# Block 1's projections as Strassen pairs ahead of attention, its gates kept in DRAM

## The reference

```python
u = _rmsnorm(h, norm_mix_g[l])
z = jnp.einsum('bsd,dn->bsn', u, w_in[l])
q, k, v, pz, ga, gp = jnp.split(z, offs, axis=-1)      # 768, 768, 768, 768, 1024, 1024 columns
a = _attention_branch(q, k, v).astype(dt)              # 12 heads of 64, dilations 1, 4, 16
p = _pool_branch(pz, w_pool_grp[l], pool_scale[l]).astype(dt)
merged = (jax.nn.sigmoid(ga) * jnp.einsum('bsc,cd->bsd', a, w_att_out[l])
          + jax.nn.sigmoid(gp) * jnp.einsum('bsc,cd->bsd', p, w_pool_out[l]))
h = h + jnp.einsum('bsd,de->bse', merged, w_out[l])
```

## Time and profile before

| what | value |
|---|---|
| median of 3 runs | 2798.54 us (2798.17 to 2798.96) |
| span of the profiled execution | 2796.0 us |
| PE busy | 2786.1 us (100%), 13352 matmuls |
| DVE, ACT, POOL busy | 1735.9, 1323.9, 188.6 us |
| chain that ended last | PE 98% |
| DMA | 302.75 MB, mean 108 GB/s |

### The profile page before, as it was taken

How to read it: one execution, slowest core, us unless ns; L and a number is a source line. 1 busy time by engine, 2 the same in 40 slices (tenths; PEclk the granted TensorE clock), 3 DMA queues, 4 the chain that set the end, 5 groups by cost and what they waited for, 6 DMA issues and landing times.

```text
span 2796.0 us, 34960 instructions
## 1 busy us (share of the span) xinstructions
PE 2786.1 (100%) x13352; PEld 2280.6 (82%) x13352; DVE 1735.9 (62%) x2477; ACT 1323.9 (47%) x2101; POOL 188.6 (7%) x133
## 2 busy tenths in 40 slices
PE   9999999999999999999999999999999999999998
PEld 8888878888888888888777788888888888888887
DVE  5344465335866667679766524998245866666786
ACT  5444452124655554444455414887123655544452
POOL 1223410000000000000132200000000000000000
PEclk9999999999999999999999999999999999999999
DMA  3111111223343475542311121212123443384442
GB/s 129 38 38 39 38 46 46 59 69 121 136 154 152 151 263 207 174 117 88 137 54 54 46 61 53 61 53 61 45 68 136 147 154 151 136 330 159 155 136 72
DMA packets 86126, 302.75 MB, mean 108 GB/s; under 512 B 9552, under 2 KB 9680, under 8 KB 79696
## 3 DMA queue, kind: packets, MB, share of 16 engines
q1 hardware_dynamic: 84672, 295.88, 31.0%
q10 hardware_dynamic: 1296, 4.72, 0.6%
HBM read 225.07 MB, written 75.50 MB: 107 GB/s over the span
## 4 chain that ended last, share of the span: by engine, by line
PE 98%; issue 1%; DVE 1%; DMA 0%; ACT 0%; POOLq 0%; POOL 0%; SPq 0%; DVEq 0%
PE ps L405 25%; PE ps L2524 17%; PE pa L2890 11%; PE ps L2890 11%; PE ps L2919 9%; PE pa L2919 9%; PE pa L405 4%; PE ps L2937 3%; PE ps L2751 3%; PE pa L2602 2%; PE pa L2647 2%; PE pa L2613 1%; PE pa L2625 1%; PE pa L2573 1%; PE pa L2751 0%
## 5 line engine op out<-in xcount | busy, mean ns | idle before, releaser
L395 DVE TENSOR_TENSOR w_lo<-w_raw,w_hi 128x1024 fp32r<-128x1024 f32 x134 | 161.4, 1205 | 429.6 <-ACT w_hi L389 429.5
L389 ACT ACTIVATE w_hi<-w_raw 128x1024 fp32r<-128x1024 f32 x134 | 137.8, 1029 | 412.0 <-PE ps L405 260.6
L405 PE MATMUL ps<-a_hi,w_hi 128*128 128x512 f32 x896 | 276.3, 390 | 0.0
L405 PE MATMUL ps<-a_lo,w_hi 128*128 128x512 f32 x896 | 275.9, 389 | 0.0
L405 PE MATMUL ps<-a_hi,w_lo 128*128 128x512 f32 x896 | 275.9, 389 | 0.0
L1259 ACT ACTIVATE krh<-k_rraw 128x512 fp32r<-128x512 f32 x192 | 121.1, 631 | 229.9 <-PE ps L2919 117.0
L2524 PE MATMUL ps<-a_hi,w_hi 128*128 128x512 f32 x672 | 223.2, 413 | 0.4 <-DVE a_lo L1766 0.4
L2046 DVE TENSOR_TENSOR krl<-k_rraw,krh 128x512 fp32r<-128x512 f32 x192 | 132.5, 690 | 132.2 <-ACT krh L1259 131.8
L2524 PE MATMUL ps<-a_lo,w_hi 128*128 128x512 f32 x672 | 209.2, 392 | 0.0
L2524 PE MATMUL ps<-a_hi,w_lo 128*128 128x512 f32 x672 | 208.4, 391 | 0.0
L405 PEld LDWEIGHTS ps<-a_hi,w_hi 128*128 128x128 f32 x896 | 167.8, 188 | 37.2 <-issue 2.5
(11 more groups left out here) (377 smaller groups left out, 6102.8 us busy)
## 6 DMA issues: line engine op xcount, KB each, us to landing
w_raw<-wstream SPq DMA_DIRECT2D x134, 512.0 KB, 3.5
k_rraw<-hff SPq DMA_DIRECT2D x224, 256.0 KB, 2.8
hff<-hbuf SPq DMA_DIRECT2D x32, 1024.0 KB, 3.9
wA<-wff SPq DMA_DIRECT2D x16, 2048.0 KB, 8.0
hff<-hbuf SPq DMA_DIRECT2D x32, 768.0 KB, 3.3
w_raw<-wff SPq DMA_DIRECT2D x32, 512.0 KB, 4.4
f_raw<-wff SPq DMA_DIRECT2D x32, 512.0 KB, 4.5
hres<-zt SPq DMA_DIRECT2D x16, 512.0 KB, 2.6
```

Source lines behind the costliest of these rows:

```text
L389: nc.scalar.activation(w_hi[:, slot, 0:n], w_raw[:, slot, 0:n], ACT.Copy).then_inc(s_whi, 1)
L395: nc.vector.tensor_tensor(w_lo[:, slot, 0:n], w_raw[:, slot, 0:n], w_hi[:, slot, 0:n].bitcast(F32), ALU.subtract).then_inc(s_wlo, 1)
L405: mm = nc.tensor.matmul(out[0:m, c], w[0:kp, slot, wofs:wofs + m], x[0:kp, k, c * HC:(c + 1) * HC], start=first and n == 0, stop=last and ...
```

## The change

Block 1's q, k, v and pooling inputs become 12 Strassen pairs that run before attention. Each output is multiplied by `rb` on POOL and stored to a DRAM tensor `proj`; SP loads it back when attention or the pooling wants it. All 16 gate units move ahead: four (`N_START`) in the start in the place of v0, q0, k0, v1, and twelve as the fill of attention, now 12 matmuls a step up to step 39 and 6 after. DVE multiplies a gate out of PSUM by `rb`, ACT takes tanh, SP stores it to DRAM `gates`; in mrg1 they are loaded back into `gslot`. mrg1 has no projection left: rows, six mix outputs, eight pooling products, eight att_out. In PE's `fill`, gate unit m waits until gate m - 2 is out of PSUM (`s_gev`); a mix output waits for the `mixed_lo` of the output two before it, and the first pooling product for five of the six. The rest of the kernel only has other counts in its waits. The diff, cut to its core:

```diff
-        return 24 if s < 40 else 12
+        return 12 if s < 40 else 6
@@ ACT, start: after the squares
+            def first_units():
+                act.wait_ge(s_mm, 1)
+                nc.scalar.activation(gate_at(0), pair_flat(0), ACT.Copy).then_inc(s_outA, 1)
+                split_hi(act, 2, 0, 1, 1)
+                for k in range(4):
+                    scaled_input(k)
+                copy_rb(0)
+                split_hi(act, 3, 1, 1, 2)
+                t_hi(T1)
+                for k in range(4, KT):
+                    scaled_input(k)
+                gate_tanh(0)
+                gate_tanh(1)
+                proj_hi(0, 0)
+                proj_hi(0, 1)
+                gate_tanh(2)
+                t_hi(T3)
+                t_hi(T2)
...
+                t_hi(T4)
+                proj_hi(0, 2)
+                proj_hi(0, 3)
+                gate_tanh(3)
+                for n in range(4, 7):
+                    proj_hi(0, n)
+            def projections():
+                for i in range(LASTP):
+                    for n in range(7):
+                        if n in (0, 1, 4):
+                            proj_copy(i, n, n)
+                        elif n == 2:
+                            proj_first(i, n)
+                        proj_hi(i + 1, n)
...
@@ DVE, start
+                split_lo(dve, 2, 0, 1)
+                rms(0)
+                split_lo(dve, 3, 1, 2)
+                gate_out(0)
+                t_sum(T1)
+                gate_out(1)
+                proj_sum(0, 0)
+                t_lo(T1)
+                gate_out(2)
+                t_sum(T3)
+                t_sum(T2)
+                proj_lo(0, 0)
+                proj_lo(0, 1)
+                t_sum(T4)
+                proj_sum(0, 1)
+                proj_lo(0, 2)
+                proj_lo(0, 3)
+                gate_out(3)
...
@@ PE
+                        elif m >= 2:
+                            pe.wait_ge(sem("s_gev"), m - 1)
+            def projections():
+                for i in range(N_PROJ):
+                    for at, n in enumerate(LAST_ORDER if i == LASTP else range(7)):
+                        pe.wait_ge(sem("s_olo"), 7 * i + n + 1)
+                        if n in (2, 3, 6):
+                            copied = {2: 3, 3: 1, 6: 2} if i == LASTP else {2: 1, 3: 2, 6: 3}
+                            pe.wait_ge(sem("s_pcp"), 3 * i + copied[n])
...
+            keep_busy(26)
+            fill(1, 0, 96)
+            stats(0)
+            fill(1, 96, 120)
+            broadcast(0)
+            fill(1, 120, 48 * N_START)
+            projections()
             attention(1)
...
             rows(0)
             rows(1)
+            for sb in range(2):
+                mix(sb)
+            for n in range(6):
+                pool_out(n)
             pe.wait_ge(sem("s_alo"), 2)
+            for n in range(KT):
+                att_out(n)
+            for n in (6, 7):
+                pool_out(n)
@@ ACT, one attention step
+                    if done is not None:
+                        unit_hi(done)
+                    if s in PHI_STEPS:
+                        pool_hi(PHI_STEPS[s])
+                    if 2 <= s < NS1 + 2:
+                        probs_pair(s - 2)
+                    for hh in range(2):
+                        if s < NS1:
+                            exp(2 * s + hh)
+                        if hh == 0 and s >= 7 and (s - 7) % 4 == 0:
+                            o_out((s - 7) // 4)
...
+                    if done is not None:
+                        gate_tanh(done)
@@ ACT, mrg1
+            for n in range(3):
+                row_out(n)
+            mixed_hi(0)
+            for n in range(3, 6):
+                row_out(n)
+            mixed_hi(1)
+            row_exp(0)
+            row_exp(1)
+            mixed_hi(2)
+            row_exp(2)
+            unit_split(U_PO[0])
+            for i in range(3, 6):
+                mixed_hi(i)
...
@@ DVE, mrg1
             dve.wait_ge(sem("s_rowc"), 3)
             link(nc.vector.tensor_tensor(mmin[:], mrow[0][:], mrow[1][:], ALU.min))
             link(nc.vector.tensor_tensor(mmin[:], mmin[:], mrow[2][:], ALU.min))
+            mixed_lo(0)
             for g in range(3):
                 nc.vector.tensor_tensor(mrow[g][:], mrow[g][:], mmin[:], ALU.subtract).then_inc(sem("s_rowd"), 1)
+            mixed_lo(1)
...
+            mixed_lo(2)
...
+            unit_split(U_PO[0])
+            mixed_lo(3)
+            reciprocal_of_sum(0)
+            mixed_lo(4)
+            reciprocal_of_sum(1)
+            mixed_lo(5)
+            unit_split(U_PO[1])
```

More of the change, by code:

```diff
@@ new lines, in _ @@
+            sp.wait_ge(sem("s_prod1"), 7 * LASTP + 3)
+            for p in range(2):
+                qk_load(p)
+                v_load(p)
+            for t in range(2):
+                z_load(t)
+            proj_store(LASTP)
+            for t in range(2, 4):
+                z_load(t)
+            for m in range(N_START, N_GATE):
+                load_unit(sp, m + 2, m % 2)
+                gate_store(m)
+                if m % 2 and m < 13:
+                    p = (m - 1) // 2
+                    qk_load(p)
+                    v_load(p)
+                    if p == 5:
+                        z_load(4)
+                        z_load(5)
@@ L556, in _ @@
+            load_unit(sp, 27, 1)
+            for n in range(2):
+                sp.wait_ge(sem("s_mrg"), n + 1)
+                gate_load("p", 6 + n, 6 + n)
+            for u in (28, 29):
+                load_unit(sp, u, u % 2)
             out_stage(1, xT)
@@ L702, in windows @@
                 nc.gpsimd.memset(tick[:], 0.0).then_inc(sem("s_wsum"), 1)
[L704 to L720, removed]
+            for t in range(NPOOL):
+                pool.wait_ge(sem(f"s_ldz{t % 2}"), 16 * (t // 2 + 1))
+                windows(t)
             for c in range(2):
@@ new lines, in proj_copy @@
+            def proj_copy(i, n, at):
+                act.wait_ge(sem("s_prod1"), 7 * i + at + 1)
+                if i and n == 4:
+                    act.wait_ge(sem("s_fc"), 3 * i - 1)
+                elif i:
+                    act.wait_ge(sem("s_u2" if n == 0 else "s_p75"), i)
+                elif n == 4:
+                    act.wait_ge(sem("s_xl"), KT + 4)
+                else:
+                    act.wait_ge(sem("s_bc"), 1)
+                dst, src = {0: (p_p1[:], 0), 1: (p_p5[:], 2), 4: (p_p7, 3)}[n]
+                nc.scalar.activation(dst, proj_bank(i, src), ACT.Copy).then_inc(sem("s_pcp"), 1)
@@ new lines, in add_max @@
+                    dve.wait_ge(s_add, j + 1)
+                    nc.vector.tensor_reduce(stat(negm, 1, j), sm1[:, j % 4, 0:w], axis=AXX, op=ALU.max,
+                                            negate=True).then_inc(s_max, 1)
+                for s in range(END1):
+                    done = unit_at(1, s - 1) if s else None
+                    if done is not None:
+                        split_lo(dve, done + 2, done % 2, done + 1)
+                    if s < NS1:
+                        add_max(2 * s)
+                        add_max(2 * s + 1)
+                    if done is not None:
+                        gate_out(done)
+                    if next_operand(s, OP_STEP + 1):
+                        first_operand_lo(*next_operand(s, OP_STEP + 1))
+                    if s + 1 in PHI_STEPS:
+                        pooled(PHI_STEPS[s + 1])
+                    if s in PLO_STEPS:
+                        pool_lo(PLO_STEPS[s])
@@ L3054, in weight_stream @@
     w = i["w_in"][0]
-    first = {"v": 12, "q": 0, "k": 6, "z": 18, "ga": 24}
-    for kind, n in ATT1_UNITS:
-        out[:, u] = tiles(w, first[kind] + n)
+    for kind, n in GATES:
+        out[:, u] = tiles(w, {"a": 24, "p": 32}[kind] + n)
         u += 1
@@ L3125, in out_units, with projection_weights @@
     return u
+def projection_weights(w):
+    first = {"v": 12, "q": 0, "k": 6, "z": 18}
+    out = np.zeros((P, N_PROJ, 2, KT, P), np.float32)
+    for j, (kind, n) in enumerate(P_UNITS):
+        out[:, j // 2, j % 2] = tiles(w, first[kind] + n)
+    return out.reshape(P, N_PROJ, 2, S)
 def hidden_weights(*ws):
```

1204 lines of the change are left out of this document (709 added, 495 removed).

## The result

The changed kernel takes 2803.76 us (median of 11 runs, 2801.47 to 2807.10) against 2798.54 before (11 runs, 2798.01 to 2799.30): ratio 1.0019, 95% interval 1.0011 to 1.0027. It is slower by some 5 us where 9.7 us of gain were forecast.

A forecast was written before the change was run, and what follows sets the result against it. PE was taken to bound the kernel, busy 2786.1 of 2796.0 us. -32.6 + 7.4 + 0 + 3 + 10.5 + 2 = -9.7 gave span 2786.3, and 2788.8 with the median's 2.5 us; range 2775 to 2802.

The forecast's parts named there:

- What is taken away: Block 1's projections: 144 fewer matmuls at 226.7 ns each, saving 32.6 us.
- Start: 7.4 us: Start before the pairs: PE waits 2.4 us for the second gate and 5.0 us for product 2's copy.
- Pairs: 0: The 12 Strassen pairs: 19.04 us of PE each covers DVE, ACT, POOL and stores, cost 0.
- Into attention: 0: Loads of q, k, v for head pair 0 behind the last pair: 0 to 3 us, taken as 0.
- Attention: "I take 3": Attention with halved fill: covered up to step 40, then waits in the last steps, taken as 3 us.
- the 198: Attention stage without waits: about 198 us, from 328.1 less 130 for 12 units.
- The bound of 8: Upper bound on attention's waits: 3 us twice over and a late window sum, 8 us.
- an in-order step of ACT that the halved fill no longer covers: Rival in attention: two steps need over 8.4 us, 2809 at 9.4 a pair; chance 0.14 together with slower pairs.
- mrg1: 10.5 us: mrg1: PE waits for DVE's mixed_lo between rows and pooling, and before pool_out(6); sum 10.5 us, bounds 8 and 15.
- The clock: 2: Low clock behind the start's 5.0 us wait adds 2 us, between 0 and 4; 0 in mrg1.
- the first rival's waits: Rival that the saving arrives nearly whole: start and mrg1 less rigid, waits 8 to 14 us, 2774 to 2781; chance 0.17.
- The prediction's 0.45: Time in us of one matmul on PE at the 1.2 GHz clock.

The follow-up runs named there:

- g1: f4 with gate 1 back behind T1's sum, the second start copy early too, and the edits of g2 and g4: 2779.28 us, ratio to before 0.9929.
- f1: Changed kernel with ACT's gate tanh one step later and SP loading weights ahead of gate stores: 2793.49 us, ratio to before 0.9976.
- g2: f1 plus the fifth window mean on DVE four steps earlier: 2790.01 us, ratio to before 0.9968.
- e4: Changed kernel plus 48 matmuls of no use in PE's known waits, in the start and mrg1: 2800.84 us, ratio to before 1.0010.
- g4: Changed kernel with f3's mrg1 order, plus third pooling output's product and weight split between the reciprocal's halves: 2796.57 us, ratio to before 0.9990.
- e1: Changed kernel with ACT's tanh of a finished gate issued one step later in attention: 2804.81 us, ratio to before 1.0021.
- e3: Changed kernel with mrg1's six mix outputs done as they come on ACT and DVE, row work in the gaps: 2809.61 us, ratio to before 1.0040.
- f3: e3's mrg1 order plus pooling weights loaded ahead of the gates' loads and an earlier split for pooling output 1: 2803.32 us, ratio to before 1.0014.
- f4: Changed kernel with early start copy, gate 1 ahead of T1's sum, late tanh, loads first and f3's mrg1 order: 2789.01 us, ratio to before 0.9964.
- e2: Changed kernel with ACT's copy for product 2 of pair 0 issued ahead of the tanh of gate 3: 2799.40 us, ratio to before 1.0006.
- f2: Changed kernel with SP loading weights ahead of gate stores, tanh left in place: 2796.96 us, ratio to before 0.9993.

## Why the prediction was wrong

- **What is taken away.** Right. 13208 matmuls; g1, whose waits in the changed stages are 10.4 us, ends 17.1 us under the span of before. The saving is real and was lost again to waits.
- **Start: 7.4 us.** Right: 2.4 and 4.8 us at the two places named. A wait of 0.8 us for the last pair's copy (290.7 us) was not walked.
- **Pairs: 0.** Right: no other wait from 80 to 290 us, PE busy for 209.88 of 210.
- **Into attention: 0.** Right for q, k and v (ACT waits 1.0 us for them, PE not at all). But I counted only these loads. The store of the last pair also holds SP, with the weights of unit 6 behind it; it made the first and longest wait in attention.
- **Attention: "I take 3".** This is the step that failed: 211.0 us where 201 were walked, with waits of 10.2 us. Of these 2.5 stand in the last steps, about what the 3 was for; the 7.5 for `vtok` had no term at all. I walked the loop from transposes over maximum and exponential and found 5 us of slack. I did not walk the other loop, from a finished unit over split, bias, gate product and tanh to the first `vtok` copy, though `V_STEP` had moved so that this copy stands right behind the tanh. The other 2.8 us over the 198 are slow matmuls and remainders (both below). The bound of 8 was too low as well. What I had as a rival, an in-order step of ACT that the halved fill no longer covers, is that mechanism, but in one step of eight, not in all, and with SP as a member, which the rival left out. f1 removes it, and g2 then measures 201.1 us, the walk's own number: engines with enough time, in a bad order.
- **mrg1: 10.5 us.** Right in place and nearly in size: stage 126.2 us for 125.6, waits 8.0.
- **The clock: 2.** Right where it was priced (e4: 2.0 us in the start) and right in mrg1 (0). I left out attention. There the same wait had two outcomes. The changed kernel waits 2.62 us for `vtok` at 458.5 us, g4 waits 2.56 us at 458.7; the next ten microseconds, of the changed kernel and of g4, are

```profile
460.00:470.00 10.00, 9.98 (x77) 7.86 (x76) 4.86 (x12) 7.13 (x18) 0.02 (x1) 1.00 0.18 57
```

```profile
460.00:470.00 10.00, 10.00 (x49) 7.64 (x49) 3.57 (x11) 4.63 (x14) 0.14 (x2) 0.66 0.20 61
```

  49 matmuls in place of 77, and `rows(0)` 3.3 us later. The profiled execution of the changed kernel ran at the fast end of its own 11 runs; the median is 1.8 us above it, and g4 shows what a run that is less lucky loses. The Trainium skill, TensorE: Matmul & The Clock Gate, "HAM oscillation", describes a kernel that waits some 3 to 5 us for DMA between its bursts of matmuls, and each burst behind such a wait starts cold. The wait of 4.8 us in the start agrees (0.50). That section has no wait as short as 2.6 us; here low clock behind such a wait cost 3.3 us in g4 and nothing in the changed kernel.
- **Remainders.** Without their waits the stages of g1 are 0.9 to 1.5 us longer than walked (pairs 1.5, attention 1.3, mrg1 0.9, the rest 0.9). Some of it in attention is low clock (0.58 in 480 to 484 us of g1); the rest was not traced. Three sums of the prediction are slightly off and decide nothing: 12 units are 130.6 us, not 130; two steps less 24 fill matmuls are 8.2 us by the rows, not 8.4 (g2 has 8.5 without a stop); the first rival's waits give 2774 to 2780, not 2781.

So my mechanism for the gain and four of five prices were right, and one missed loop of 7.5 us, its clock, and 2 to 3 us of small ones turned a gain of 10 into a loss of 5.

## What to carry to other kernels

When a change shortens the cover of a loop, walk every loop that the cover hid, once around and across all queues, DMA issue queue too: the one that broke here ran over four engines and a load that stood behind a store. Put what somebody waits for soon (small copies, loads) ahead of what nobody needs soon (stores, and the tanh that feeds them), and take a wait away only after asking which instruction stands behind the one you move: e1, e3, f3 and f4 each uncovered the next.

## What the hardware showed beyond that

- Whether the clock falls behind a stop of PE differs between executions with the same code there. Behind the 2.40 us stop of the start the stretch 46 to 58 us has 1.00 in ten of the twelve profiled executions that have it, and 0.86 in the other two, e2 and f2. Behind the stop of 2.5 to 2.7 us near 458 us, 460 to 470 us has 1.00 in the changed kernel, e2, e3 and e4 and 0.66 in f3 and g4. Length alone does not decide: the 1.84 us stop before the scores of the last steps left the clock at 1.00 in e2 and g3, and the changed kernel has 0.61 behind it; g1's stops of 1.0 us together near 480 us had 0.58 behind them. The changed kernel's runs spread over 5.6 us, those of before, with waits of 1.0 us at most, over 1.3; g1's over 2.4. Of the changed kernel's 11 runs the four fastest have a mean granted clock of 0.996 to 0.997 and the three slowest 0.994. So the clock goes with the spread; that it makes all of it is not shown, nor what decides.
- In the low stretch of e2 (50.56 to 53.12 us) a 128x512 matmul follows the last after 0.427 us, at full clock after 0.227: 1.88 times, not twice. The prediction's 0.45 was the double.
- A clock of 0.72 (520 to 524 us) cost nothing in mrg1, where each stop ends on DVE: the price of a slow matmul is that of the slack behind it.
- A weight split on DVE beside POOL's window sum took 2.51 us, 1.22 alone. POOL's small operation beside it took 1.17 us, 0.19 alone. DVE's gate product, which reads one operand from PSUM, kept its 1.21 us beside POOL.
